# Moving three modulation units in TensorE's order around the second norm, the affinities and the token rows

## What is computed

```python
def expert_choice_ffn(h, w_router, w_gate, w_up, w_down):
    cap = CAPACITY_FACTOR * S // N_EXPERTS                       # 32 tokens for each expert
    aff = softmax(einsum('bsd,de->bse', h, w_router), axis=-1)   # affinities
    gate, idx = lax.top_k(swapaxes(aff, 1, 2), cap)
    xe = h[bidx, idx]
    a, u = xe @ w_gate, xe @ w_up
    ye = (silu(a) * u) @ w_down
    return zeros_like(h).at[bidx, idx].add(gate[..., None] * ye)

# each layer of the first block
h = h + hybrid_mixer(rmsnorm(h, norm_mix[l]), ...)
h = h + expert_choice_ffn(rmsnorm(h, norm_ffn[l]), ...)

# the second block needs, of its conditioning vectors alone:
def adaln(cvec, w, b):
    m = silu(cvec) @ w + b                                       # w is 1024 x 6144
```

## Time and profile before

| | us |
|---|---|
| median of three runs | 2124.45 |
| lowest, highest | 2123.13, 2127.17 |
| the profiled execution, its own time | 2125.11 |
| its span in the profile | 2123.0 |
| PE busy | 1917.3 (90%) |
| DVE busy | 641.3 (30%) |
| ACT busy | 546.9 (26%) |

### The profile page before, as it was taken

How to read it: one execution, slowest core, us unless ns; L and a number is a source line. 1 busy time by engine, 2 the same in 40 slices (tenths; PEclk the granted TensorE clock), 3 DMA queues, 4 the chain that set the end, 5 groups by cost and what they waited for, 6 DMA issues and landing times.

```text
span 2123.0 us, 31497 instructions
## 1 busy us (share of the span) xinstructions
PE 1917.3 (90%) x13966; PEld 1171.1 (55%) x13966; DVE 641.3 (30%) x988; ACT 546.9 (26%) x856; POOL 0.2 (0%) x4
## 2 busy tenths in 40 slices
PE   9999998787878999998998989889999998889887
PEld 8988833131312898883333434349999744434443
DVE  4576500000000558650241111038668300000001
ACT  4466300000000447620210222034554211011102
POOL 0000000000000000000000000000000000000000
PEclk9999999999999999999999999999999999999999
DMA  9735999999999962599999999983426999999997
GB/s 359 267 128 181 393 416 427 428 427 428 428 428 421 373 235 105 208 390 414 428 424 419 417 424 420 428 346 131 166 101 237 405 427 428 428 427 428 427 428 302
DMA packets 123007, 748.18 MB, mean 352 GB/s; under 512 B 6288, under 2 KB 27152, under 8 KB 83344
## 3 DMA queue, kind: packets, MB, share of 16 engines
q1 hardware_dynamic: 122896, 746.52, 86.2%
HBM read 745.45 MB, written 1.05 MB: 352 GB/s over the span
## 4 chain that ended last, share of the span: by engine, by line
PE 57%; DMA 36%; DVE 3%; ACT 2%; issue 1%; SPq 0%; DVEq 0%; ACTq 0%
PE bank L878 13%; DMA ring<-w_expert_up 12%; DMA ring<-moe_w_up 11%; PE bank L969 10%; DMA ring<-w_expert_down 9%; PE bank L1022 9%; PE bank L881 5%; DMA ring<-w_expert_gate 4%; PE bank_pair L819 4%; PE bank_pair L822 2%; PE bank L1000 2%; PE bank L905 1%; PE bank L1189 1%; PE bank L839 1%; PE bank L1210 1%
## 5 line engine op out<-in xcount | busy, mean ns | idle before, releaser
L969 PE MATMUL bank<-ring,arena 128*32 128x512 f32 (+1 forms) x2848 | 489.7, 526 | 88.4 <-DMA ring<-w_expert_up 40.1
L969 PEld LDWEIGHTS bank<-ring,arena 128*32 128x32 f32 x2848 | 146.9, 110 | 397.4 <-issue 206.7
L1022 PE MATMUL bank<-ring,arena 128*32 128x512 f32 x1408 | 307.1, 610 | 44.6 <-DMA ring<-w_expert_down 36.7
L1022 PEld LDWEIGHTS bank<-ring,arena 128*32 128x32 f32 x1408 | 75.6, 112 | 253.2 <-issue 186.1
L1875 ACT ACTIVATE arena<-bank 128x512 f32<-128x512 f32 (+1 forms) x130 | 66.9, 542 | 452.4 <-PE bank L984 217.4
L2451 DVE TENSOR_TENSOR arena<-arena,bank 128x512 f32<-128x512 f32 x24 | 15.8, 686 | 549.9 <-PE bank L969 549.9
L878 PE MATMUL bank<-extra_parts,ring_parts 128*128 128x256 f32 x1024 | 169.5, 282 | 0.0
L878 PEld LDWEIGHTS bank<-extra_parts,ring_parts 128*128 128x128 f32 x1024 | 140.3, 188 | 6.7 <-ACT arena_parts L1875 2.7
L878 PE MATMUL bank<-ring_parts 128*128 128x256 f32 x672 | 127.3, 283 | 2.1 <-DVE ring_parts L2878 1.1
L969 PE MATMUL bank<-arena 128*32 128x256 f32 (+1 forms) x832 | 110.8, 441 | 8.9 <-DMA arena<-moe_w_gate 5.7
L819 PE MATMUL bank_pair<-extra_parts,arena_parts 128*128 128x512 f32 x320 | 109.7, 396 | 0.0
(11 more groups left out here) (389 smaller groups left out, 2353.8 us busy)
## 6 DMA issues: line engine op xcount, KB each, us to landing
ring<-w_expert_down SPq DMA_DIRECT2D x62, 2048.0 KB, 23.7
ring<-w_expert_gate SPq DMA_DIRECT2D x58, 2048.0 KB, 21.8
ring<-w_expert_up SPq DMA_DIRECT2D x54, 2048.0 KB, 25.6
ring<-w_in SPq DMA_DIRECT2D x32, 2048.0 KB, 13.5
ring<-moe_w_up SPq DMA_DIRECT2D x24, 2048.0 KB, 34.1
arena<-moe_w_gate SPq DMA_DIRECT2D x20, 2048.0 KB, 36.3
ring<-moe_w_down SPq DMA_DIRECT2D x20, 2048.0 KB, 33.7
ring<-ada_w SPq DMA_DIRECT2D x12, 2048.0 KB, 17.8
```

The costliest lines, as they stand in the source:

```text
L969: last = pe.matmul(to[own_rows(half, e)].rearrange("p (q c) -> p q c", c=own), x_slots[:, c, 32 * e:32 * e + 32], w[:, k, half], start=c = ...
L1022: last = pe.matmul(banks[4 + e // PAIRS][own_rows(half, e), :].rearrange("p (x d) -> p x d", x=2), hidT[:, e // PAIRS * own + f % own, own ...
```

## The change

Only PE's program changes, at one place that each of the two layers runs through once.

```diff
+                ada_unit(ADA_HEAD)
                 router_part(3)
-                ada_unit(ADA_HEAD)
                 token_rows(0)
+                ada_unit(ADA_HEAD + 1)
                 pe.wait_ge(dve_done, dve_at("aff", loops))
                 out = take(2, "dve", "aff rows")
                 for half in range(TH):
                     last = pe.transpose(out[0:EXPERTS, half * P:(half + 1) * P], aff[:, half, :], ident)
                 last.then_inc(pe_done, pe_p.mark("aff rows"))
-                for n in range(ADA_HEAD + 1, ADA_UNITS):
-                    ada_unit(n)
                 for j in (2, 1, 3):
                     token_rows(j)
+                ada_unit(ADA_HEAD + 2)
+                idle_products(take(0, "act", "router exp"), 8, ones)
                 pe.wait_ge(dve_done, dve_at("idx diag 0", loops))
```

## The result

The changed kernel takes 2131.38 us (median of 13 runs, 2124.93 to 2133.87), the kernel before 2124.93 in the same comparison (13 runs, 2122.01 to 2127.17). The ratio is 1.0027, 95% interval 1.0019 to 1.0035: **slower by 0.27%**, where 2122.8 (2120.0 to 2125.4) was predicted. The profiled execution has an own time of 2133.49 and a span of 2131.4, 8.4 longer than before.

What follows compares the result with a forecast made beforehand. The kernel was taken to alternate between PE work and weight transfers (57% and 36% of the chain). Gains of 1.59 and 1.83 us sum to 3.42; one clock fall leaves 1.7, giving 2122.8 us, range 2120.0 to 2125.4.

Steps and rivals of the forecast that it cites:

- costed at nothing: Behind the affinities: token-row transposes, unit 5 and filling products, together 5.23 us, hidden beside DVE's 6.25 us chain.
- late at the slot tokens: Rival: filling products and unit 5 make PE late to the slot tokens, 4.2 us per layer; 2129.5, chance 0.07.
- 1.59 and 1.83 us earlier: DVE's copy of the affinities starts 1.59 us earlier in the first layer and 1.83 in the second.
- forecast 7.4 to 7.5: First layer, clock up: DVE's copy of the affinities starts 7.4 to 7.5 us after mix 3, against 9.05.
- the likeliest case: The clock falls in one of the two layers' passages; 2122.8 us, chance 0.38.
- the 3.42 us of the sum: Both layers' earlier affinity copies together gain 3.42 us, almost all of it from PE working at the upper clock.
- one fall in two passages: Each layer's passage has about an even chance of a clock fall, which costs 1.7 us of work.
- The hole behind unit 3: The gap in SP's weight loads is filled, load at 246.8 instead of 251.9, but a hole opens at 265.
- the shift of PE would reach the end of the layer: The weight stream shifts by PE's gain, 1.59 and 1.83 us, and the transfer-paced tile stage carries it through.
- The cover for the filling products: Ahead of the slot tokens 1.0 us of PE idle time is left, as before the change.

Runs made afterwards that it cites:

- fill_only: Kernel before with only the eight filling products per layer added behind the last token rows, no unit moved; 2131.51 us, ratio 1.0029.
- pad_only: Kernel before with 16 one-column products nobody reads between the second block's norms, layers untouched; 2128.92 us, ratio 1.0026.
- small_pad: Kernel before with 16 products of 32 by 32 columns ahead of the second block's norms, within PE's idle time; 2128.44 us, ratio 1.0016.
- no_fill: Changed kernel without its eight filling products per layer, the three units staying moved; 2131.33 us, ratio 1.0035.
- wide_fill: Changed kernel filled by two 512-column products instead of eight of 128, with six products also taken from the warm-up; 2126.14 us, ratio 1.0009.
- more_pad: Changed kernel with 48 one-column products more between the second block's norms; 2142.16 us, ratio 1.0088.
- loop_back: Changed kernel, passage word for word, with 18 products fewer elsewhere ahead of the loop, made up for by wide ones; 2125.95 us, ratio 1.0009.
- after_64: Changed kernel with 48 products of 32 by 32 columns ahead of the second block's norms, 64 more than before in all; 2125.42 us, ratio 1.0004.
- rows_only: Kernel before with only token rows 0 moved, from in front of the affinities to behind units 4 and 5; 2123.67 us, ratio 0.9994.
- unit3_only: Kernel before with only unit 3 moved ahead of the last router part, no filling products; 2124.97 us, ratio 1.0006.

## Why the prediction was wrong, point by point

**What was missed: where the loop lies.** The prediction summed what the 16 filling products take on PE (1.85 us a layer, hidden, so "costed at nothing") and forgot that they are code. One pass of the loop has 1,624 product and weight-load records in the trace and 52 others of PE that aren't counted as work. The fetches come in packets of 16 KB. The Trainium skill ("Runtime: NRT & Kernel Launch", section "Instruction fetch mechanics") says that PE keeps 128 KiB of instructions, 2,048 of them, refilled in blocks of 16 KiB, 256 instructions each. By this the loop covers seven or eight blocks, according to where it begins.
The way from packet to time goes mainly over PE's stop. The 28 packets have 0.46 MB, at the 430 GB/s of the earlier trace rows 1.1 us; as mere traffic they would explain a quarter. But PE stops for 4.5 to 4.9 us at the jump and does the gather 1.4 to 1.7 us slower. Of these about 6 us most is absorbed, since PE would have waited for its first weights anyway (2.30 and 1.09 us in the kernel before, nothing in the changed one), and 1.5 are left. The up weights then arrive that much later; how much of this is the stop and how much the somewhat slower stream (425 GB/s in that step against 427) isn't shown.

No rival held this. The one on the slower side (late at the slot tokens) was priced at 2129.5 and did not happen: PE is 1.1 us ahead of the slot tokens in both layers, where 1.0 was forecast. PE's timeline after, first layer:

```profile
258.21 2.05 PE L785 MATMUL bank<-cst 128*128 128x128 f32 x16
261.37 0.48 PE L1468 MATMUL bank<-arena,cst 16*128 16x128 f32 x2 [1.11 <-DVE arena L2829]
262.68 1.58 PE L905 MATMUL bank<-arena 128*128 128x128 f32 x12 [0.83 <-issue]
```

(The window ends at 264; all 16 records of the last line take 2.02 us.)

**The term that was mis-sized: 1.59 and 1.83 us earlier.** I compared the new order with the clock up against the old one with the clock down in both layers. Both have both cases. From mix 3 to the copy of the affinities, us, first and second layer:

| order | kernel: layers |
|---|---|
| old | before 9.05, 9.29; fill_only 9.08, 7.70; pad_only 6.09, 8.99; small_pad 9.29, 7.71 |
| new | changed 9.36, 7.70; no_fill 7.71, 9.32; wide_fill 9.31, 7.70; more_pad 7.70, 9.32; loop_back 7.71, 9.32; after_64 9.31, 7.70 |

The new order has 7.70 with the clock up (forecast 7.4 to 7.5) and 9.32 with it down, the latter in just one layer of each of the six executions, as the likeliest case said. But the old one has 6.09 when the clock stays up, since only unit 3 and the first token rows stand in it and not unit 4. The means are 8.40 (old, eight passages) and 8.51 (new, twelve). So the right term was about nothing in each layer, and the step that failed is the one that took the clock of before's two passages for a property of its order: the 3.42 us of the sum, where the means differ by 0.1 us a layer the other way. In the old order a fall can also take a part of the passage only: in the 7.70 of fill_only the sums and the router ran at full clock, and unit 3 took 3.5 us.

**The clock.** The forecast of one fall in two passages held, and also its size, 1.6 us (9.32 less 7.70; forecast 1.7). Against the rule of the Trainium skill ("TensorE: Matmul & The Clock Gate", section "HAM oscillation — how this bites in real kernels") that the prediction tells, the clock fell in stretches in which PE was busy all the time, in all six.

**The queue.** The hole behind unit 3 closed and one opened ahead of the load behind the first expert unit, as said. That the shift of PE would reach the end of the layer was only partly right. Counted from mix 3 against the kernel before, eleven layers of the runs begin their first tile over 1.3 us earlier, by 2.4 on the mean, and their last tile by 1.0. The changed kernel's own second layer keeps 1.65 of 3.2; rows_only's 2.2 there turn into 1.2 later. The five layers that begin it over 1.2 us later, by 2.0 on the mean, are 1.9 late at the last tile. One of these five is the changed kernel's first layer: the tile begins 1.9 us later than before, and 2.2 us are there at the last tile. In it the clock is lower behind the slot columns than before the change (0.75 and 0.50 against 0.88 and 0.70 in the kernel before, 278 to 286). The layers between the two groups end from 2.6 earlier to 1.3 later, so a single layer says little.

```profile
280.00:284.00 4.00, 4.00 (x70) 2.71 (x71) 2.09 (x7) 0.00 (x0) 0.00 (x0) 0.75 0.92 332
284.00:288.00 4.00, 4.00 (x14) 0.76 (x14) 0.61 (x2) 0.00 (x0) 0.00 (x0) 0.50 0.99 418
```

**The cover for the filling products** was called nothing, rightly; what they are for was not costed. In this order they are needed: without them each layer is 2.8 us longer.

**The sum, as it should have been.** Moves with the filling in, loop in place: 2126.14, 2125.95 and 2125.42 in three kernels, some 1 us above before and hardly to be told from it. The loop: 4.2 us between marks, 3.5 by the small pad's medians, 5.4 and 6.0 by the two kernels that took the packets out of the changed one. Together with the 1 us of the moves that is 4.5 to 7, measured 6.5; what lies between the 3.5 and the 6.0 stays open. Of the 8.4 us between the two profiles, the 1.5 ahead of the first passage and the 2.1 between the blocks are in code that is the same; over all the kernels run the first of these stretches varies by 2.7 us, and the second, in the kernels that have the same code in it, lies from 3.1 below before (unit3_only) to 5.5 above (fill_only, whose profiled execution was its slowest, 4.2 above its median). I put both down to scatter.

## What to carry to other kernels

Added instructions are code before they are work: where a loop on an engine covers nearly as many instructions as that engine keeps, anything put ahead of it can make it fetch itself anew in each pass. Look at the instruction queue in the table of DMA queues of both kernels, and for idle time of PE put down to "issue" at the loop's first products, before explaining a difference by the edit; if they changed, shift the loop by some harmless products, or fill with few wide ones in place of many narrow ones, and measure again. And before comparing a new order with an old one where the clock falls, find or make an execution of the old one with the clock up: otherwise the gain may be one that the old order sometimes gets by itself (three of its eight passages here took 6.1 to 7.7 us, not 9).

## What the runs showed of the hardware that I had not expected

- A loop of 1,624 product and weight-load records a pass on PE ran without a packet on the instruction queue, or with 9 packets and a stop of 4.5 to 4.9 us at each jump back, of which 1.5 us arrived, according to whether 0 or 64 instructions stood ahead of it more; 256 more were as good as none.
- The clock went down in one of two passages with the same instructions, in the same execution, in all six kernels of the new order.
- A product of one column is not small: with 128 weight columns its record took 0.113 us at the upper clock and 0.2 at the lower one (20 in 4 us of more_pad), and one of 32 by 32 columns 0.038 (1.20 us for 32). The clock fell under 96 of the former though PE was never idle.
- Of PE's gains ahead of a stretch paced by transfers 1.0 of 2.4 us was left at the layer's last tile on the mean of eleven layers, with single ones from all of it to less than nothing; of its losses 1.9 of 2.0 (five layers).
